# Two transformer blocks on one core: units by token half at the stage boundaries, two extra weight slots, values token-major

## The reference, cut to what matters

```python
def swiglu(x, w_gate, w_up, w_down):
    return (jax.nn.silu(x @ w_gate) * (x @ w_up)) @ w_down      # hidden width 2816

def hybrid_layer(x, ...):                                       # block 1
    x = x + 0.5 * swiglu(rmsnorm(x, norm_ffn1), ffn1_gate, ffn1_up, ffn1_down)
    proj = rmsnorm(x, norm_mix) @ w_in
    qa, ka, va, qb, kb, vb, g_a, g_b = parts                    # 12 and 8 heads of 64, two gates of 1024
    ...                                                         # dilated windows with logsumexp merge; MoBA
    merged = jax.nn.sigmoid(g_a) * (y_a @ w_up_a) + jax.nn.sigmoid(g_b) * (y_b @ w_up_b)
    x = x + merged @ w_out
    x = x + 0.5 * swiglu(rmsnorm(x, norm_ffn2), ffn2_gate, ffn2_up, ffn2_down)
    return x                                                    # then rmsnorm(x, norm_final)

def second_block(x, c, positions, ...):                         # block 2, depth 2
    cond = jax.nn.silu(c)
    for i in range(DEPTH_2):
        mod = (cond @ ada_w[i] + ada_b[i])[:, None, :]
        sh1, sc1, g1, sh2, sc2, g2 = jnp.split(mod, 6, axis=-1)
        h = rmsnorm_2(x, norm1_g[i]) * (1.0 + sc1) + sh1
        ...  # i = 0: sliding window, 16 query and 2 key heads, rope, sinks; i = 1: stick-breaking, 16 heads
        x = x + g1 * y
        h = rmsnorm_2(x, norm2_g[i]) * (1.0 + sc2) + sh2
        x = x + g2 * swiglu_2(h, w_gate[i], w_up[i], w_down[i])
    return x
```

## Time and profile before

| | |
|---|---|
| median of 3 runs | 1337.12 us |
| profiled execution | 1337.01 us, of which span 1334.9 us |
| TensorE busy | 1229.1 us, 92% |
| VectorE busy | 841.6 us, 63% |
| ScalarE busy | 634.4 us, 48% |
| GpSimd busy | 51.0 us, 4% |
| DMA | 253.90 MB, 190 GB/s in the mean |
| granted TensorE clock, mean | 0.964 |

### The profile page before, as it was taken

One profiled execution on the slowest core, in us unless ns is written; L12 is line 12 of the kernel. 1 busy time (PEld: TensorE's weight loads), 2 busy tenths in 40 slices (PEclk: granted clock), 3 DMA queues, 4 the chain that ended last, 5 costly groups with the idle time before them and its releaser, 6 DMA issues.

```text
span 1334.9 us, 16086 instructions
## 1 busy us (share of the span) xinstructions
PE 1229.1 (92%) x6598; PEld 1048.8 (79%) x6598; DVE 841.6 (63%) x1104; ACT 634.4 (48%) x833; POOL 51.0 (4%) x100
## 2 busy tenths in 40 slices
PE   5899997999999999999688789999969988899998
PEld 3688876999998788787586568888859977688886
DVE  3677767347538677668757578666765464644444
ACT  4433445345555434444446654433447794533332
POOL 0000000000000010001000001000000000000000
PEclk9899998999999999999788989999979999899999
DMA  7687776443344487777231048777624333355551
GB/s 291 225 319 276 270 260 221 158 163 123 107 147 169 166 330 271 259 273 272 103 117 42 32 138 304 269 272 271 221 101 159 126 111 100 139 175 185 189 189 64
DMA packets 43704, 253.90 MB, mean 190 GB/s; under 512 B 5104, under 2 KB 5488, under 8 KB 19824
## 3 DMA queue, kind: packets, MB, share of 16 engines
q1 hardware_dynamic: 28656, 200.29, 42.5%
q0 software_dynamic: 13824, 50.34, 10.3%
q10 hardware_dynamic: 1152, 2.26, 0.5%
HBM read 251.82 MB, written 1.05 MB: 189 GB/s over the span
## 4 chain that ended last, share of the span: by engine, by line
PE 80%; DVE 10%; ACT 7%; issue 2%; DMA 1%; ACTq 0%; DVEq 0%
PE ps L1202 18%; PE ps L1204 18%; PE ps L1203 18%; PE ps L1195 6%; PE ps L1196 6%; PE ps L1197 6%; ACT w_hi L376 2%; DVE w_lo L691 1%; PE ps L1281 1%; ACT junk L391 1%; DVE xn L779 1%; PE ps L1424 1%; DVE h_lo_t L787 1%; PE ps L1409 1%; DVE x L744 1%
## 5 line engine op out<-in xcount | busy, mean ns | idle before, releaser
L691 DVE TENSOR_TENSOR w_lo<-raw,w_hi 128x2048 fp32r<-128x2048 f32 x186 | 424.8, 2290 | 205.5 <-ACT w_hi L376 203.0
L376 ACT ACTIVATE w_hi<-raw 128x2048 fp32r<-128x2048 f32 x186 | 350.3, 1906 | 20.5 <-DMA raw<-in_w 20.4
L1202 PE MATMUL ps<-w_hi,h_hi_t 128*128 128x512 f32 x800 | 326.3, 408 | 32.7 <-DVE h_lo_t L787 12.1
L1204 PE MATMUL ps<-w_lo,h_hi_t 128*128 128x512 f32 x800 | 316.6, 396 | 0.0
L1203 PE MATMUL ps<-w_hi,h_lo_t 128*128 128x512 f32 x800 | 316.0, 395 | 0.0
L1195 PE MATMUL ps<-h_hi_t,w_hi 128*128 128x256 f32 x688 | 201.0, 292 | 9.0 <-DVE h_lo_t L787 7.7
L1202 PEld LDWEIGHTS ps<-w_hi,h_hi_t 128*128 128x128 f32 x800 | 153.3, 192 | 67.2 <-issue 19.6
L1196 PE MATMUL ps<-h_lo_t,w_hi 128*128 128x256 f32 x688 | 197.7, 287 | 0.0
L1197 PE MATMUL ps<-h_hi_t,w_lo 128*128 128x256 f32 x688 | 197.4, 287 | 0.0
L1204 PEld LDWEIGHTS ps<-w_lo,h_hi_t 128*128 128x128 f32 x800 | 152.9, 191 | 33.5
L1203 PEld LDWEIGHTS ps<-w_hi,h_lo_t 128*128 128x128 f32 x800 | 153.4, 192 | 32.2 <-issue 1.9
(11 more groups left out here) (160 smaller groups left out, 1108.4 us busy)
## 6 DMA issues: line engine op xcount, KB each, us to landing
raw<-in_w SPq DMA_DIRECT2D x186, 1024.0 KB, 4.9
ada_raw<-in_ada_w POOLq DMA_DIRECT2D x96, 512.0 KB, 5.0
x<-in_x SPq DMA_DIRECT2D x2, 512.0 KB, 5.9
raw<-in_w SPq DMA_DIRECT2D x4, 256.0 KB, 6.8
gate<-in_ada_b ACTq DMA_DIRECT2D x2, 512.0 KB, 11.6
gate<-in_ada_b SPq DMA_DIRECT2D x2, 512.0 KB, 6.6
out_x<-x SPq DMA_DIRECT2D x2, 512.0 KB, 2.6
const<-in_const ACTq DMA_DIRECT2D x1, 768.0 KB, 6.5
```

What stands on the lines that cost most here:

```text
L376: act.activation(w_hi[:, u % RING, :], raw[:, u % RING, :], ACT.Copy).then_inc(hi_ready, 1)
L691: V.tensor_tensor(w_lo[:, u % RING, :], raw[:, u % RING, :], w_hi[:, u % RING, :].bitcast(F32), ALU.subtract).then_inc(lo_ready, 1)
L1202: TE.matmul(dst, x_hi, wh, start=start, stop=False, skip_group_check=True)
L1204: return TE.matmul(dst, x_hi, wl, start=False, stop=last, skip_group_check=True)
```

## The change: what it does

1. **Slots.** `AHEAD` is 4. In the FFNs two more slots (one in ffn1) lie over buffers that only the attention stages use; `plan_slots` works out for each unit its slot (`SLOT`), the unit held there before (`HELD`) and the count of loads (`LOADS`). The first unit in an extra slot also waits until the split of the attention's output is done.
2. **Halves.** The last pair of an FFN runs gate and up of half 0, then down of half 0, then gate and up of half 1, then down of half 1. `rows_stage` runs four units for half 0, then for half 1. From FFN 1 on, pairs 0 and 1 run half 0 of both (four unit halves) and then half 1, and the down units and modulation products follow. `value_pass` runs the first 4 units of w_in and qkv_b for half 0, with the turn of the second half's rows in their middle, then for half 1. Adds, roots, table loads and splits are put in a new order to suit (`rows_then`, the FFN's tail).
3. **Values.** Value columns are computed token-major by `value_unit` (512 columns by `three_wide`, per token half: 256 columns), with the value units put first; `values` stays only in the stage of the sliding window.
4. **Norms without shift** (0, 1, 2): ScalarE casts from PSUM with the gain as its scale, VectorE subtracts from PSUM in one operation.
5. **Start.** x is loaded by ScalarE's queue, `const` and `vecs` by SyncE's; a table load goes first; `ada_w` starts after w slot 4's first load.

```diff
-AHEAD = 3
+EXTRA = 2
+AHEAD = 4
+def plan_slots():
...
+    for u in range(TOTAL):
+        name, i = stage_of[u]
+        allowed = list(range(RING))
+        if name.startswith("ffn") and (name == "ffn0" or i >= 1) and not 26 <= i <= 30:
+            allowed += [RING] if name == "ffn1" else [RING, RING + 1]
+        s = min(allowed, key=lambda k: (last[k], k))
...
+PASS = 4
+W_IN_ORDER = [6, 7, 8, 13, 14, 0, 1, 2, 3, 4, 5, 9, 11, 10, 12] + list(range(15, 23))
+W_IN_VALUES = 5
+QKV_B_ORDER = [8, 9, 10, 11, 0, 4, 1, 5, 2, 6, 3, 7]
...
+                if u in EXTRA_FIRST:
+                    sp.wait_ge(h_lo, H_BASE[{"ffn1": "merged", "ffn2": "y2", "ffn3": "y3"}[EXTRA_FIRST[u]]] + 8)
+                wait(sp, unit_done, HELD[u] + 1)
+                sp.dma_start(raw[SLOT[u]], inp["w"][u]).then_inc(w_loaded[SLOT[u]], 16)
...
-            pool.wait_ge(w_loaded[2], 16)
+            pool.memset(table[:, 0:1], 0.0).then_inc(zero_set, 1)
+            pool.wait_ge(w_loaded[4], 16)
... # ScalarE, ffn: the tail
+                p = PAIRS - 1
+                end = u0 + FFN_UNITS
+                hid_hi_of(p - 1, slice(0, 2 * T), hidT_count(f, p - 1) + 1)
+                hi(end)
+                silu(p, 0)
+                hid_hi_of(p, slice(0, T), hidT_count(f, p) + 1)
+                hi(end + 1)
+                if then is not None:
+                    load_table(ACT.Sqrt)
+                hi(end + 2)
+                if then == 4:
+                    norm_root(3, 0)
+                if then is not None:
+                    norm_root(then, 0)
+                    load_table(ACT.Silu)
+                silu(p, 1)
+                if then is not None:
+                    load_table(ACT.Sqrt)
+                if then is not None and then != 4:
+                    norm_hi(then, 0, 0)
+                act.wait_ge(hidlo_done, hidT_count(f, p) + 1)
+                hid_hi_of(p, slice(T, 2 * T), hidT_count(f, p) + 2)
...
+            def rows_then(stage, n):
+                u0 = BASE[stage]
+                load_table(ACT.Sqrt)
+                for j in range(3):
+                    hi(u0 + j + AHEAD)
+                norm_root(n, 0)
+                norm_hi(n, 0, 0)
+                norm_hi(n, 0, 1)
+                hi(u0 + 3 + AHEAD)
+                norm_root(n, 1)
+                load_table(ACT.Silu)
... # VectorE, ffn: the start from FFN 1 on
+                    hidden(0, 0)
+                    norm_lo(n, 1, 0)
+                    norm_lo(n, 1, 1)
+                    lo(u0 + AHEAD)
+                    hidden(1, 0)
...
+                    lo(u0 + 1 + AHEAD)
...
+                    hidden(0, 1)
+                    lo(u0 + 2 + AHEAD)
+                    hid_lo_of(0, slice(0, 2 * T), hidT_count(f, 0) + 1)
...
+                    hidden(1, 1)
+                    lo(u0 + 3 + AHEAD)
...
+                    lo(u0 + 4 + AHEAD)
+                    for k in units[4:6]:
+                        ada(k)
+                    modulation(0)
+                    modulation(1)
... # VectorE, ffn: the tail
+                for k in units[0:2]:
+                    ada(k)
+                hid_lo_of(p - 1, slice(0, 2 * T), hidT_count(f, p - 1) + 1)
+                lo(end)
+                hidden(p, 0)
+                hid_lo_of(p, slice(0, T), hidT_count(f, p) + 1)
+                lo(end + 1)
...
+                add(0)
+                lo(end + 2)
+                if then == 4:
+                    norm_rstd(3, 0)
+                    hidden(p, 1)
+                    norm_rstd(4, 0)
...
+            def rows_then(stage, n, gated=None):
+                u0 = BASE[stage]
+                for j in range(3):
+                    lo(u0 + j + AHEAD)
...
+                for h in range(2):
+                    add_to_x(stage, 0, h, None, gated)
+                norm_rstd(n, 0)
+                norm_lo(n, 0, 0)
+                norm_lo(n, 0, 1)
+                lo(u0 + 3 + AHEAD)
+                for h in range(2):
+                    add_to_x(stage, 1, h, None, gated)
+                norm_rstd(n, 1)
... # PE, ffn: pairs 0 and 1, then the last pair
+                    gate_up(0, 0, 0)
+                    gate_up(0, 1, 0)
+                    turn_x(n, 1)
+                    gate_up(1, 0, 0)
+                    gate_up(1, 1, 0)
+                    gate_up(0, 0, 1)
+                    gate_up(0, 1, 1)
+                    gate_up(1, 0, 1)
+                    turn_hid(0, (0, 1))
+                    gate_up(1, 1, 1)
+                down_all(0)
+                mod_job(0)
+                mod_job(1)
...
+                down(p - 1, 0, 0)
+                turn_hid(p, (0,))
+                down(p - 1, 0, 1)
+                pe.wait_ge(hidlo_done, hidT_count(f, p) + 1)
+                for h in range(2):
+                    down(p, 0, h, True).then_inc(acc_done, 1)
                 gate_up(p, 0, 1)
                 gate_up(p, 1, 1)
...
+                if then is not None and then != 4:
+                    turn_x(then, 0)
+                down(p - 1, 1, 0)
+                turn_hid(p, (1,))
+                down(p - 1, 1, 1).then_inc(unit_done, 1)
+                if then == 4:
+                    turn_x(then, 0)
```

More of the change, by code:

```diff
@@ L42 @@
     TOTAL += _n
+def plan_slots():
+    stage_of = {}
+    for name, n in STAGES:
+        for i in range(n):
+            stage_of[BASE[name] + i] = (name, i)
+    last, loads = [-1] * (RING + EXTRA), [0] * (RING + EXTRA)
+    slot, before, count = [], [], []
+    for u in range(TOTAL):
[4 more added lines that the diff above has]
+        s = min(allowed, key=lambda k: (last[k], k))
+        slot.append(s)
+        before.append(last[s])
+        last[s] = u
+        loads[s] += u > 0
+        count.append(16 * loads[s])
+    return slot, before, count
+SLOT, HELD, LOADS = plan_slots()
+EXTRA_FIRST = {u: name for name in ("ffn1", "ffn2", "ffn3")
+               for u in [min(u for u in range(BASE[name], BASE[name] + FFN_UNITS) if SLOT[u] >= RING)]}
 H_BASE, _t = {}, 0
@@ L813, in ffn @@
+            def ffn(f, n, then, factor=None, gated=None):
                 late = f < 2
@@ new lines, in ffn @@
+                lo(end + 1)
+                if gated is not None:
+                    dve.wait_ge(mod_read, 2 * (6 * (f - 2) + GATE[1]) + 2)
+                if then is not None and then not in UNSHIFTED:
+                    dve.wait_ge(modg_done, {4: 1, 6: 3}[then])
+                add(0)
+                lo(end + 2)
+                if then == 4:
+                    norm_rstd(3, 0)
+                    hidden(p, 1)
+                    norm_rstd(4, 0)
+                elif then is not None:
+                    norm_rstd(then, 0)
+                    for k in units[2:3]:
+                        ada(k)
+                    hidden(p, 1)
+                    norm_lo(then, 0, 0)
+                else:
+                    hidden(p, 1)
@@ new lines, in ffn @@
+                hid_lo_of(p, slice(T, 2 * T), hidT_count(f, p) + 2)
+                if then == 4:
+                    norm_lo(4, 0, 0)
+                if then is not None:
+                    norm_lo(then, 0, 1)
+                if then == 4:
+                    for k in units[2:3]:
+                        ada(k)
+                add(1)
+                lo(end + 3)
+                if then == 4:
+                    norm_rstd(3, 1)
+                    norm_rstd(4, 1)
+                elif then is not None:
+                    norm_rstd(then, 1)
```

667 lines of the change are left out of this document (330 added, 337 removed).

## The result

The changed kernel takes 1344.12 us (median of 5 runs, 1342.84 to 1345.57) beside 1337.12 us for the kernel before in the same series: ratio 1.0055, 95% interval 1.004 to 1.007. The forecast was 1333.3 and faster: the sign is wrong. The time lies above the forecast's own range (1329 to 1340) and inside the whole one (1319 to 1345). The profiled execution has a span of 1342.1 us, before 1334.9.

The account below looks back on a forecast made before the run. TensorE (PE), busy 92% of the span, was taken as the bound, so only its gaps and the slow matmuls behind them counted. Terms summed to -3.7 us from 1337.0, giving 1333.3; own range 1329 to 1340, whole range 1319 to 1345.

Parts of the forecast that it names:

- step 2: FFN 0 to w_in: half 0's down products cover half 1's boundary work; minus 7.5 us, bounds minus 9 and minus 4.
- step 3: Token-major values: 36 transposes and nine copies go, five waits of 0.8 come; minus 1 us, bounds minus 5 and plus 3.
- step 4: w_out to FFN 1: a late weight split leaves PE 7.7 us idle; plus 6 us, bounds plus 9 and minus 3.
- step 7: Starts of FFN 1 to 3: VectorE's queue delays the second modulation product; plus 7.7, plus 8 and plus 1.3 us.
- step 5: FFN 1 to qkv_a: PE gaps of 5.9, 10.6 and 10 us; plus 13 us, bounds plus 16 and 0.
- step 6: wo_a to FFN 2 and wo_b to FFN 3: 2 us idle remain; minus 6 us each, bounds minus 7 and 0.
- step 8: FFN 2 to qkv_b: as FFN 0 to w_in, without ada; minus 12.4 us, bounds minus 14 and minus 6.
- step 1: Start: with vecs landing at 7.2, unit 2 starts at 32.3 instead of 39.4; minus 7 us, bounds minus 8 and minus 1.
- "wrong": Signs against the forecast: gaps at L1281 in FFN 0 and 2 over 2 us, or the angles' end not holding PE.
- The rival of late hidden products at every FFN end: Half 1's hidden product 3 us later at the ends of FFN 0 and 2: plus 5 each, 1343 us; chance 0.16.
- The rival of VectorE keeping up: The modulation product gaps of FFN starts vanish: minus 15.7, 1317.6 us, or 1325 if half goes; chance 0.15.
- The rival of drains: Six added table switches at three FFN ends cost 8.3 us more in all, about 1342 us; chance 0.03.

Follow-up runs that it names:

- the run with the split moved: Changed kernel, FFN 1's first pairs only: casts and splits of pair 0's hidden tile put ahead of the third unit ahead's split: 1343.68 us, ratio 1.0055.
- the modulation edit: Changed kernel with FFN 1 to 3's second modulation product issued 24 matmuls later and VectorE's reading of the first ahead of two ada steps: 1327.95 us, ratio 0.994.
- the ada edit: Changed kernel with the second of two ada steps in an FFN's last pair put behind half 0's hid split: 1341.97 us, ratio 1.0042.
- FFN 1's end mended: Changed kernel, FFN 1's end: third unit's split behind half 1's hid split; fourth split and last ada step behind all half 1's normalised rows: 1331.57 us, ratio 0.9954.
- all edits: Changed kernel with all edits except stick-breaking's, plus the fourth split behind half 1's root in wo_a and wo_b: 1282.81 us, ratio 0.9599.

## Why the prediction was wrong

**Failed: step 2, "VectorE does two ada steps instead of one before the hid split, which comes 0.8 late".** The step's busy time was counted, and not that its piece comes by a DMA into one of three buffers. That buffer's last reader and its new issue are these:

```profile
190.62 1.28 DVE L815 SCALAR_TENSOR_TENSOR ada_acc<-ada_raw,cond,ada_acc 128x1024 f32<-128x1024 f32 x1
192.19 0.53 POOL L409 DMA_DIRECT2D ada_raw<-in_ada_w  x1 [3.04 <-DVE ada_acc L815]
```

It was free at 191.9 us, and the step that needs the new piece started at 200.1, 8.2 us later; from issue to landing it took some 7.9 us, where 5.1 is the median of these loads. That made the gap 3.58 where 0.8 was said, with 1.7 us of slow matmuls behind it (24 and a turn in 7.4 us). The other two gaps of step 2 came smaller: none before the hid turn (1.3 was said) and 0.73 for the hid copy (1.4). From pair 9's hid turn to w_in's start the time fell by 3.7 us and not by 6.6. This is 2.9 of the 3.9 missed in the stretch. Most of the rest is in w_in, where step 3 priced the transposes too high (below). That the experiment's 4.1 is close to 3.9 is chance: it also takes away the 0.8 that was forecast, and brings a gap of 1.16.

**Mis-sized: steps 4 and 7 in FFN 1.** The gap of 7.49 came as forecast (7.7), that before the modulation product was 5.30 instead of 4.3. The first hid split, put at about 1, was 1.97, and the sum charged no slow matmuls to a gap below 2 us: here 24 took 7.23 us where they take 5.60 in FFN 2. These three, 1.0 + 1.0 + 1.6, make the 3.6 missed. Two smaller errors about cancel: FFN 1 began 0.7 sooner than forecast, and the gap of before that goes was credited with 5.9 us and was 3.24 with 1.6 of slow matmuls. The first two gaps are one thing: a queued unit that comes late, which shows at whichever product of VectorE PE needs next, as the run with the split moved showed. That the single extra slot of FFN 1 makes it late is argued, not shown. The modulation waits of FFN 1 to 3 are worth 16.2 us by the experiment, where step 7 had 17.0 for them and the first hid splits together. The 2.4 us charged for slow matmuls behind every gap of 3 us or more was somewhat high: 1.7, 1.9 and 1.5 us stand behind the gaps at 202, 481 and 833.

**Mis-sized: step 3.** A transpose was priced by busy time, 0.14 each. Matmuls overlap, and the trace of before has four of them in 0.36 us of PE's time:

```profile
1027.16 0.60 PE L1380 MATMUL ps<-const,qkv 128*128 128x128 f32 x4
1027.52 0.36 PE L1195 MATMUL ps<-h_hi_t,w_hi 128*128 128x256 f32 x1
```

All 36 that went took 3.5 us from the first of a group to the next matmul, 0.10 each, and not 5.0: 0.9 less in w_in and 0.6 in the stick-breaking stage. The four waits of z there were right (3.3 where 3.2 was said). Waits for softplus, which the step left at nothing, grew by 0.6 (5.7 us, before 5.1). And behind the gap of 3.24 us that both kernels have at the stage's end, matmuls ran slow for 5.9 us where before it was 3.4, some 1.2 us of time. Together this is the 2.7. No edit has shown what part of the slow matmuls goes back to the new order of the steps; that stays open.

**Right:** steps 5, 6 and 8. For step 5 experiments show the mechanism; for 6 and 8 it is only that size and place of the gaps came as said. Step 1 missed 1 us: vecs, taken to land at 7.2, landed at 5.7 (4.5 us after its issue), but the first matmul then stood for the split of the first weights until 11.79 and not 10.8, a case that its bounds had. Nearly every sign named for "right" came, the gaps of 8, 6, 10, 10 and 4 to 5 us, and none of those for "wrong": they tested the steps and not the sum. The rival of late hidden products at every FFN end (1343) came near the time by chance: the gaps before FFN 0's and 2's hid turn of half 1 are below 0.3 us. The rival of VectorE keeping up did not come by itself, but the modulation edit shows that it could: its waits were order, not work. The rival of drains is out: the 16 table loads of L440 have 3.3 us idle before them in all, 3.1 of it ahead of the very first at the start. By the Trainium skill (ScalarE: Activation LUTs, What ACT_TABLE_LOAD costs) each would have a drain of 1.38 us; the trace doesn't show it.

```profile
L440 ACT ACT_TABLE_LOAD x16 | 20.5, 1283 | 3.3 <-issue 3.1
```

**The forecast's size.** The terms came to -40 and +36 us. With nine terms of 6 to 13 us a net of -3.7 is no more than a sign drawn from their errors; the chances of 0.56 and 0.25 said too little of that.

## What to carry to other kernels

When an order written by hand is changed, look at each engine's queue for what stands between a short critical operation and its engine: a weight split whose slot comes free late, a small DMA-fed side job, a second product into a bank that is still being read. Moving such items turned +0.5% into -4.0% without touching the computation, and only with the two extra slots. Ask of a side job that reads a DMA's buffer when its piece lands: here it held the queue for 3.02 us beside 1.28 of work. Price removed matmuls by the time from one start to the next (0.10 us here), not by their busy time (0.14). And where large gains and losses nearly cancel, forecast the parts and leave the sign open.

## What was not expected of the hardware

The lower clock costs an amount that the gap before it does not fix. After FFN 1's end the attention stage ran the same matmuls in all kernels; in these four behind gaps of 9.46, 9.21, 7.64 and 7.65 us. Windows from the turn to wo_a's start, of the changed kernel, the one with the ada edit, the one with FFN 1's end mended and the one with all edits:

```profile
676.20:773.50 97.30, 75.90 (x478) 67.20 (x479) 63.84 (x188) 59.41 (x144) 0.00 (x0) 0.86 0.16 55
```

```profile
672.50:770.90 98.40, 78.95 (x479) 70.17 (x479) 63.79 (x188) 59.46 (x144) 0.00 (x0) 0.82 0.16 54
```

```profile
661.40:757.70 96.30, 72.80 (x479) 64.43 (x479) 69.36 (x192) 60.42 (x145) 0.53 (x1) 0.88 0.18 61
```

```profile
627.03:724.08 97.05, 75.36 (x479) 66.76 (x479) 69.40 (x191) 60.50 (x145) 0.53 (x1) 0.86 0.17 60
```

PE's busy time for it is 75.90, 78.95, 72.80 and 75.36 us at a granted clock of 0.86, 0.82, 0.88 and 0.86. The stage itself differs less, by 2.1 us from 96.30 to 98.40, for part of the longer matmuls falls into waits: the one before the scores at 718.5 us is 2.30 us in the changed kernel, 1.85 with the ada edit and 5.04 with FFN 1's end mended. No edit changes PE's work in the stage, and what sets the level no run shows. Executions of one kernel differ as well: the four with the modulation edit took 1325.85 and 1326.61 us at mean clocks of 0.972 and 0.973, and 1329.3 and 1330.05 at 0.966 and 0.967. So an edit that is worth less than some 2 us can't be read from the total, only from its own stretch. The start varies too: PE's second unit begins at 33.2 us in the profile of the changed kernel and 1.2 earlier in that of the ada edit, whose start is the same; over the ten kernels with this start, pair 1's hid turn in FFN 0 lies between 56.2 and 58.3 us.
